# First attention layer: two heads of a chunk per job, score calls alternating between row halves and value calls between column halves

## What is computed

```python
# 16 query heads of 64 in 4 groups, one key and value head each; blocks of 128 queries
s_loc = einsum(q, k_of_3_blocks) * scale      # previous, own and next block, |distance| <= 128
s_loc = where(mask, s_loc, -inf)
s_ctx = einsum(q, k_context) * scale          # 256 context keys
p = softmax_with_sink(concatenate([s_loc, s_ctx]), sink)   # the sink's column is dropped after
ox = einsum(p[..., :384], v_of_3_blocks) + einsum(p[..., 384:], v_context)
# context queries attend to the context keys alone, with the sink
yx = (ox * silu(gx)) @ w_out                  # the same for the context
```

## Time and profile before

| | us |
|---|---|
| median of 3 runs | 3017.63 |
| lowest and highest run | 3004.48 to 3023.93 |
| the profiled execution | 3006.76 |
| its span, first to last instruction | 3005.4 |
| TensorE busy in the span | 2782.4 (93%) |
| DVE busy | 1707.1 (57%) |
| ACT busy | 1022.9 (34%) |

### The profile page before, as it was taken

How to read it: one execution, slowest core, us unless ns; L and a number is a source line. 1 busy time by engine, 2 the same in 40 slices (tenths; PEclk the granted TensorE clock), 3 DMA queues, 4 the chain that set the end, 5 groups by cost and what they waited for, 6 DMA issues and landing times.

```text
span 3005.4 us, 33845 instructions
## 1 busy us (share of the span) xinstructions
PE 2782.4 (93%) x12834; PEld 2170.3 (72%) x12834; DVE 1707.1 (57%) x3509; ACT 1022.9 (34%) x1662; POOL 319.8 (11%) x219
## 2 busy tenths in 40 slices
PE   6779999999999989999999996999999967999997
PEld 4657888988888879999999963986444655544445
DVE  4759777666666646767775454213555443154453
ACT  3222333333333323333333333222444332244442
POOL 0110344440000012212220000000000000000000
PEclk9989999999999999999999998998999988999998
DMA  5435444445656688989996520111000111100001
GB/s 214 154 112 192 166 145 146 142 162 196 223 199 220 210 288 294 312 283 313 311 313 224 183 77 21 50 59 33 1 1 1 35 35 57 58 24 16 9 1 56
DMA packets 147553, 415.95 MB, mean 138 GB/s; under 512 B 13568, under 2 KB 75136, under 8 KB 144448
## 3 DMA queue, kind: packets, MB, share of 16 engines
q1 hardware_dynamic: 128960, 346.67, 33.6%
q0 software_dynamic: 18432, 67.12, 6.6%
HBM read 352.62 MB, written 60.82 MB: 138 GB/s over the span
## 4 chain that ended last, share of the span: by engine, by line
PE 85%; issue 6%; DVE 5%; ACT 2%; POOL 2%; DMA 0%; SPq 0%; DVEq 0%; ACTq 0%; POOLq 0%
PE psum L447 7%; PE psum L449 7%; PE psum L448 7%; PE psum L334 6%; PE psum L336 6%; PE psum L335 6%; PE psum L326 6%; PE psum L328 6%; PE psum L327 6%; PE psum L420 4%; PE psum L564 3%; PE psum L707 3%; PE psum L557 2%; PE psum L677 2%; PE psum L318 2%
## 5 line engine op out<-in xcount | busy, mean ns | idle before, releaser
L1074 DVE TENSOR_TENSOR weights_low<-arena,weights_high 128x1024 fp32r<-128x1024 f32 x290 | 355.1, 1225 | 568.6 <-ACT weights_high L756 568.0
L756 ACT ACTIVATE weights_high<-arena 128x1024 fp32r<-128x1024 f32 x355 | 374.6, 1055 | 581.6 <-PE psum L449 416.3
L334 PE MATMUL psum<-x_high,weights_high 128*128 128x448 f32 x1024 | 381.5, 373 | 16.4 <-DVE weights_low L1074 9.2
L447 PE MATMUL psum<-hidden_high,weights_high 128*128 128x448 f32 x1024 | 374.6, 366 | 1.9 <-issue 1.9
L335 PE MATMUL psum<-x_low,weights_high 128*128 128x448 f32 x1024 | 375.1, 366 | 0.0
L336 PE MATMUL psum<-x_high,weights_low 128*128 128x448 f32 x1024 | 375.1, 366 | 0.0
L449 PE MATMUL psum<-hidden_high,weights_low 128*128 128x448 f32 x1024 | 373.9, 365 | 0.0
L448 PE MATMUL psum<-hidden_low,weights_high 128*128 128x448 f32 x1024 | 373.9, 365 | 0.0
L326 PE MATMUL psum<-x_high,weights_high 128*128 128x512 f32 x776 | 318.5, 410 | 39.9 <-DVE x_low L1088 20.9
L327 PE MATMUL psum<-x_low,weights_high 128*128 128x512 f32 x776 | 309.7, 399 | 0.0
L328 PE MATMUL psum<-x_high,weights_low 128*128 128x512 f32 x776 | 309.2, 398 | 0.0
(11 more groups left out here) (213 smaller groups left out, 4172.3 us busy)
## 6 DMA issues: line engine op xcount, KB each, us to landing
arena<-in_stream SPq DMA_DIRECT2D x227, 512.0 KB, 3.5
arena<-in_v_rows SPq DMA_DIRECT2D x128, 512.0 KB, 4.9
hidden<-arena SPq DMA_DIRECT2D x128, 224.0 KB, 2.7
router<-arena SPq DMA_DIRECT2D x14, 2048.0 KB, 8.3
arena<-hidden SPq DMA_DIRECT2D x128, 224.0 KB, 5.2
arena<-router SPq DMA_DIRECT2D x16, 1792.0 KB, 13.7
arena<-in_ada_w SPq DMA_DIRECT2D x48, 512.0 KB, 3.5
arena<-in_pair_w SPq DMA_DIRECT2D x8, 576.0 KB, 3.8
```

The source lines that it names most:

```text
L334: PE.matmul(bank[b][:, 0:N], wh[u % 2][:, k, :], xh[:, k, PICKED:T], start=k == 0, stop=False)
L447: PE.matmul(out, wh[w][:, n, :], hh[:, r, :], start=e == 0, stop=False)
L756: ACT.activation(wh[u % 2], slots[u % RING], AF.Copy).then_inc(*tick("weights_high", u))
L1074: DVE.tensor_tensor(wl[u % 2], slots[u % RING], wh[u % 2].bitcast(F32), ALU.subtract).then_inc(*tick("weights", u))
```

## The change

The jobs are dealt anew: jobs j and j + 1 are the two heads of a chunk at one query tile. `a_scores(j)` issues for both heads the context keys, then the near keys, then the masks, with each call in the other row half than the call before, and signals once at the end. It waits for both exponentials of the pair before, since each head now owns one score area. `a_turn(j)` transposes for both heads, after the scores of the next pair and the value pieces, the first four tiles of a head into bank 4 or 5 and the fifth into bank 7. `a_weigh(i, piece)` issues a piece for both heads, that is for partitions 0 to 63 and 64 to 127 of the output in turn; pieces 0 and 1 come with tile 1, 2 and 3 with tile 2, 4 and 5 with tile 3, 6 and 7 with tile 5. Pieces 6 and 7 write bank 6 and so wait for the gate of the first 512 queries. There are four probability buffers in place of three and two sets of `local_t` and `far_t` per chunk. ACT makes both exponentials of the next pair before the copies of this one; with three near tiles the context part is copied in two instructions. DVE normalises a pair, then takes the maxima of the next; the sink is copied for tile 0 alone; the gates are taken in two parts at different times. The second attention layer keeps its order.

```diff
@@ -216,12 +216,13 @@
     tmp = area(90, T)
     qr = [columns_at(8 * T + c * TC, TC) for c in range(5)] + [columns_at(72 * T + c * TC, TC) for c in range(2)] + [
         columns_at(88 * T, TC)]
-    prob = [columns_at(first * T, 641) for first in (36, 38, 46)]
-    local_t = [area(48, 4 * 3 * P), area(54, 4 * 3 * P)]
-    far_t = [area(51, 2, TC), area(57, 2, TC)]
+    prob = [columns_at(first * T, 641) for first in (36, 38, 46, 90)]
+    local_t = [[area(48, 4 * 3 * P), area(54, 4 * 3 * P)], [area(25, 4 * 3 * P), area(60, 4 * 3 * P)]]
+    far_t = [[area(51, 2, TC), area(57, 2, TC)], [area(28, 2, TC), area(68, 2, TC)]]
     mask_r = rounded("mask_rounded", 24, T)
     SC = [psum[:, 0:2 * T], psum[:, 2 * T:4 * T]]
     PT = psum[:, 4 * T:6 * T]
+    A_PT = [bank[4], bank[5]]
     def a_job(j):
-
-        head, t = divmod(j, TC // P)
-        return head // 2, head % 2, t
+        i, rest = divmod(j, 2 * (TC // P))
+        return i, rest % 2, rest // 2
 
...
-    A_PIECES = [0, 2, 2, 2, 1, 1]
+    A_PIECES = [(), (0, 1), (2, 3), (4, 5), (), (6, 7)]
...
         def a_scores(j):
-            i, half, t = a_job(j)
+            i, _, t = a_job(j)
             p = i % 2
-            rows = slice(64 * half, 64 * half + 64)
-            qs = qr[i][rows, t * P:(t + 1) * P]
             lo, tiles = a_tiles(t)
-            sc = SC[j % 2]
-            if j >= 2:
+            both = [(SC[half], slice(64 * half, 64 * half + 64)) for half in range(2)]
+            if j:
                 PE.wait_ge(*at("exped", ("a", j - 2)))
-            if j == 0:
+                PE.wait_ge(*at("exped", ("a", j - 1)))
+            else:
                 PE.wait_ge(*at("mask_r", 0))
                 for n in range(8):
                     PE.wait_ge(*at("roped", ("q", n)))
+            for sc, rows in both:
+                last = PE.matmul(sc[:, T:TC], qr[i][rows, t * P:(t + 1) * P], kt[rows, p, T:TC], start=True, stop=True)
             if t < NT:
                 first = tiles[0]
-                PE.matmul(sc[:, lo:T], qs, kt[rows, p, first * P:(tiles[-3] + 1) * P], start=True, stop=False)
                 skip = (first - t + 1) * P
-                PE.matmul(sc[:, lo:T], mask_r[:, 3 * P:4 * P], mask_r[:, skip:skip + T - lo], start=False, stop=True)
-            PE.matmul(sc[:, T:TC], qs, kt[rows, p, T:TC], start=True, stop=True).then_inc(*tick("scored", ("a", j)))
+                for sc, rows in both:
+                    PE.matmul(sc[:, lo:T], qr[i][rows, t * P:(t + 1) * P], kt[rows, p, first * P:(tiles[-3] + 1) * P],
+                              start=True, stop=False)
+                for sc, rows in both:
+                    last = PE.matmul(sc[:, lo:T], mask_r[:, 3 * P:4 * P], mask_r[:, skip:skip + T - lo], start=False,
+                                     stop=True)
+            last.then_inc(*tick("scored", ("a", j)))
+
+
+        def a_turn(j):
+            n = len(a_tiles(a_job(j)[2])[1])
+            if j:
+                PE.wait_ge(*at("prob_t", ("a", j - 2)))
+                PE.wait_ge(*at("prob_t", ("a", j - 1)))
+            for half in range(2):
+                PE.wait_ge(*at("normed", ("a", j + half)))
+                for b in range(n):
+                    out = A_PT[half][:, b * P:(b + 1) * P] if b < 4 else bank[7][:, half * P:(half + 1) * P]
+                    last = PE.transpose(out, prob[(j + half) % 4][:, b * P:(b + 1) * P], K("ident"))
+            last.then_inc(*tick("prob_turned", ("a", j)))
 
...
-        def a_weigh(head, piece):
-            i, half = head // 2, head % 2
-            kv = 2 * (i % 2) + half
-            rows = slice(64 * half, 64 * half + 64)
-            local, far = local_t[head % 2], far_t[head % 2]
+        def a_weigh(i, piece):
             if piece == 0:
-                PE.wait_ge(*at("prob_t", ("a", head * 6 + 5)))
-                if i and half == 0:
-                    PE.wait_ge(*at("a_gated", (i - 1, 0)))
-            if piece == 6 and i and half == 0:
-                PE.wait_ge(*at("a_gated", (i - 1, 1)))
-            if piece < 2 or piece >= 6:
-                j = piece % 2
-                v = vt[:, 4 + j, kv * 64:(kv + 1) * 64]
-                if piece < 2:
-                    PE.matmul(bank[6][rows, :], v, far[:, j, 0:T], start=j == 0, stop=False)
+                for half in range(2):
+                    PE.wait_ge(*at("prob_t", ("a", 12 * i + 10 + half)))
+                if i:
+                    PE.wait_ge(*at("a_gated", (i - 1, 1)))
+            elif piece == 6:
+                PE.wait_ge(*at("a_gated", (i, 0)))
+            for half in range(2):
+                kv = 2 * (i % 2) + half
+                rows = slice(64 * half, 64 * half + 64)
+                local, far = local_t[i % 2][half], far_t[i % 2][half]
+                if piece < 2 or piece >= 6:
+                    j = piece % 2
+                    v = vt[:, 4 + j, kv * 64:(kv + 1) * 64]
+                    if piece < 2:
+                        last = PE.matmul(bank[6][rows, :], v, far[:, j, 0:T], start=j == 0, stop=False)
+                    else:
+                        last = PE.matmul(bank[6][rows, 0:C], v, far[:, j, T:TC], start=j == 0, stop=j == 1)
                 else:
-                    last = PE.matmul(bank[7][rows, 0:C], v, far[:, j, T:TC], start=j == 0, stop=j == 1)
-                    if j == 1:
-                        last.then_inc(*tick("weighed", ("a", head)))
-            else:
-                j = piece - 2
-                t0, t1 = max(0, j - 1), min(NT, j + 2)
-                cols = local[:, j * 3 * P + (t0 - j + 1) * P:j * 3 * P + (t1 - j + 1) * P]
-                PE.matmul(bank[6][rows, t0 * P:t1 * P], vt[:, j, kv * 64:(kv + 1) * 64], cols, start=False, stop=j == 3)
+                    j = piece - 2
+                    t0, t1 = max(0, j - 1), min(NT, j + 2)
+                    cols = local[:, j * 3 * P + (t0 - j + 1) * P:j * 3 * P + (t1 - j + 1) * P]
+                    last = PE.matmul(bank[6][rows, t0 * P:t1 * P], vt[:, j, kv * 64:(kv + 1) * 64], cols, start=False,
+                                     stop=j == 3)
+            if piece in (5, 7):
+                last.then_inc(*tick("weighed", ("a", i, piece // 7)))
 
         a_scores(0)
-        a_scores(1)
-        for j in range(A_JOBS):
-            head, t = divmod(j, TC // P)
-            turn("a", j, prob, len(a_tiles(t)[1]))
+        for j in range(0, A_JOBS, 2):
+            i, _, t = a_job(j)
             if j + 2 < A_JOBS:
                 a_scores(j + 2)
-            if head:
-                for piece in range(sum(A_PIECES[:t]), sum(A_PIECES[:t + 1])):
-                    a_weigh(head - 1, piece)
+            if i:
+                for piece in A_PIECES[t]:
+                    a_weigh(i - 1, piece)
+            a_turn(j)
         for piece in range(8):
-            a_weigh(15, piece)
+            a_weigh(7, piece)
 
...
         def a_turn(j):
             i, half, t = a_job(j)
-            head = 2 * i + half
             lo, tiles = a_tiles(t)
             near = len(tiles) - 2
-            ACT.wait_ge(*at("prob_turned", ("a", j)))
-            if t == 0 and head >= 2:
-                ACT.wait_ge(*at("weighed", ("a", head - 2)))
+            local, far, pt = local_t[i % 2][half], far_t[i % 2][half], A_PT[half]
+            if half == 0:
+                ACT.wait_ge(*at("prob_turned", ("a", j)))
+                if t == 0 and i >= 2:
+                    ACT.wait_ge(*at("weighed", ("a", i - 2, 1)))
             if near:
                 first = tiles[0] * 2 * P + (t + 1) * P
-                where = local_t[head % 2][:, first:first + near * 2 * P].rearrange("p (n c) -> p n c", c=2 * P)[:, :, 0:P]
-                ACT.activation(where, PT[:, 0:near * P].rearrange("p (n c) -> p n c", c=P), AF.Copy)
-            ACT.activation(far_t[head % 2][:, :, t * P:(t + 1) * P],
-                           PT[:, near * P:(near + 2) * P].rearrange("p (n c) -> p n c", c=P), AF.Copy).then_inc(
-                               *tick("prob_t", ("a", j)))
+                where = local[:, first:first + near * 2 * P].rearrange("p (n c) -> p n c", c=2 * P)[:, :, 0:P]
+                ACT.activation(where, pt[:, 0:near * P].rearrange("p (n c) -> p n c", c=P), AF.Copy)
+            there = far[:, :, t * P:(t + 1) * P]
+            if near < 3:
+                last = ACT.activation(there, pt[:, near * P:(near + 2) * P].rearrange("p (n c) -> p n c", c=P), AF.Copy)
+            else:
+                ACT.activation(there[:, 0, :], pt[:, 3 * P:4 * P], AF.Copy)
+                last = ACT.activation(there[:, 1, :], bank[7][:, half * P:(half + 1) * P], AF.Copy)
+            last.then_inc(*tick("prob_t", ("a", j)))
 
         a_exponents(0)
         a_exponents(1)
-        for j in range(A_JOBS):
-            a_turn(j)
+        for j in range(0, A_JOBS, 2):
             if j + 2 < A_JOBS:
                 a_exponents(j + 2)
+                a_exponents(j + 3)
+            a_turn(j)
+            a_turn(j + 1)
 
...
```

(32 more changed lines are left out.)

21 lines of the change are left out of this document (10 added, 11 removed).

## The result

| | before | changed |
|---|---|---|
| median of the runs beside each other | 3020.17 us (3004.48 to 3023.93, 4 runs) | 2934.45 us (2925.97 to 2941.94, 4 runs) |
| profiled execution | 3006.76 | 2934.38 |
| first score pass to last gate, in it | 288.5 | 215.8 |

The ratio is 0.9729, 95% interval 0.9695 to 0.9763: faster by 2.7%.

The account below looks back on a forecast made before the run. TensorE's queue was taken to bound the stage; six chunks (-42.6), chunk 0 (-1.6) and the end (-7.5) gave -51.7 us with full overlap, taken as -47 from the 3017.6 median: 2970 us, range 2948 to 3003.

Parts of the forecast that it names:

- What bounds the kernel, and the change from TensorE to the loop: First attention stage: TensorE's queue bounds before; afterwards scores, maxima, exponentials and back through one score buffer set most steps.
- the number of slots that overlapped passes take: Score and value passes of a head pair: four calls of two passes take five slots instead of eight.
- the upper bound: Most overlap thought possible: a call's last pass runs beside the next call's first, giving 26.7 us per chunk against 33.78.
- The 4.7 us that I took off the full overlap: Whole stage: allowance for weight loads shown at calls, taking the full-overlap total of -51.7 us to -47.
- The six chunks: From value group to value group: each chunk 26.7 us instead of 33.78, together -42.6 us.
- Chunk 0: First score pass to first value group, without values to hide the loop, at 1.2 GHz: 52.6 against 54.2 us, -1.6.
- The end: From the value group of chunk 7 to the last gate: 24.2 us against 31.7, -7.5.
- The offset to the median: Whole run: before's profiled execution took 3006.8 us against a median of 3017.6; the saving was subtracted from that median.
- (a): Rival: passes of opposite halves do not overlap at all; +3 us, 3020; chance 0.11.
- (b): Rival: only one kind of half, rows or columns, overlaps; about -30 or -20 us, 2988 to 2998; chance 0.09.
- (c): Rival: clock falls in each chunk's thin stretch (tiles 4, 5, 0), 5.5 us a chunk, 3004, or 2985 at half; chance 0.12.
- (d): Rival: the stage stays at 1.2 GHz, a chunk some 43.5 us; +65 us, 3083; chance 0.06.

Follow-up runs that it names:

- e1: Changed kernel with the score calls written head by head (context and near of head 0, then of head 1) instead of alternating: 2935.57 us.
- e2: Changed kernel with a tile's value calls written head by head instead of alternating: 2939.13 us.
- e5: Changed kernel plus four products of 512 columns, results unread, ahead of the first score pass: 2941.34 us.
- e6: Changed kernel plus four unread products ahead of the first score pass and two more in each step of chunk 0: 2935.44 us.
- e9: Changed kernel with a signal per head, value pieces spread over all six steps, and unread products at the start and in chunk 0: 2928.07 us.
- e11: The changed kernel run once more, unaltered, for a second trace: runs of 2929.63 to 2958.86 us, the trace being that of the longest.
- e7: Changed kernel with the second head's score passes made to wait until the first head's have ended: 3022.85 us.

## Why the prediction was wrong in size

**What bounds the kernel, and the change from TensorE to the loop: right.** The loop that I read from the earlier trace rows came out to within 0.05 us. From the end of the block to the next context pass it is 4.93 - 1.73 = 3.20 at tile 0 (3.15 put), 4.63 - 1.50 = 3.13 at tile 5 (3.16) and 2.63 - 0.63 = 2.00 at tile 4 (2.04). The waits stand where I put them, released by ACT's exponential. One wait that I had not put is ahead of the transposes of tile 4, 0.71 behind ACT's copy (L976), and lies inside the loop's time.

**The term that was mis-sized: the number of slots that overlapped passes take.** A slot is the time of one pass. I called five slots for eight passes the upper bound, from the assumption that only the last pass of a call runs beside the first of the next. Measured are four: the two passes of each pair start 7 to 42 ns apart at a full clock, and e1 and e2 show that their calls need not be neighbours in the program. So my bound was none. A block is 0.63, 1.50 or 1.73 us, not 0.84, 1.71 or 2.17, and values 0 and 1 are 1.87, not 2.28. With four slots my own steps give 1.73 + 3.15 = 4.88, 1.73 + 1.86 + 1.25 = 4.84, 1.50 + 2.77 = 4.27, 0.63 + 1.22 + 1.03 = 2.88, 0.63 + 2.04 = 2.67 and 1.50 + 3.16 = 4.66, in all 24.2, and the trace has 24.23 where I put 26.7. In six chunks that is 6 x 2.5 = 15 us of the miss. The 4.7 us that I took off the full overlap (-47 for -51.7), for weight loads shown at each call, were not there either (value passes of one half follow each other at 0.43 us, as the stream alone would have it). The Trainium skill (TensorE: Matmul & The Clock Gate, Part 3, on packing small matmuls) says that matmuls of different strips run concurrently, which 7 ns between two starts confirms. Its rule that a weight load overlaps only when its rows differ does not hold here: the two heads' value weights have the same rows, and their loads are hidden (one runs from 2166.796 to 2166.933, within the pass from 2166.794 to 2167.386).

**The six chunks.** They took 150.0 us between first and last value group, against 202.7. At 24.2 each it would have been 145.4. The clock gave back 4.6 us. So this part is -52.7, put at -42.6.

**Chunk 0: the sign right, the size wrong.** 42.7 us, put at 52.6. I had it at 1.2 GHz all through, for I read from the earlier trace rows that only value passes end the slow phase. The row of after has 0.67: the clock rose at 2088.6, in the transposes behind a block, before any value pass. It fell and rose twice more, and the thin steps of tiles 3 and 4 ran at 2.4 GHz (2.62 each where I put 3.6).

```profile
2074.90:2088.60 13.70, 9.24 (x31) 6.02 (x32) 6.44 (x18) 4.43 (x12) 0.00 (x0) 0.50 0.00 0
2088.60:2092.00 3.40, 1.50 (x15) 1.30 (x15) 3.01 (x8) 2.27 (x7) 0.00 (x0) 1.00 0.00 0
```

The rest is slots: a full step at 1.2 GHz took 6.48, not 7.15. This part is -11.5, put at -1.6.

**The end.** 23.2 us from the last chunk's value group to the last gate, put at 24.2: -8.5, put at -7.5. The stage's miss of 25.7 us is then 10.1 in the chunks, 9.9 in chunk 0, 1.0 here and the 4.7 taken off.

**The offset to the median.** The profiled execution of before lay 10.9 us below the median, and I carried this over. That of after took 2934.38, its own median. This made the other 10 us of the miss beside the stage's (-72.7 in place of -47). Two parts vary most from execution to execution. One is the front: in the thirteen traces of kernels with the change it ends between 2073.3 and 2086.6 us, with the same code in it but for the four products at its end in e5, e6 and e9 (without those three, 2073.3 to 2085.9). The windows from 1200 to 1600 us of the changed kernel's two traces, the first with its front at 2073.8, the second at 2084.6:

```profile
1200.00:1600.00 400.00, 400.00 (x1975) 370.74 (x1974) 281.07 (x343) 126.12 (x165) 80.77 (x76) 1.00 0.90 304
```

```profile
1200.00:1600.00 400.00, 400.00 (x1937) 363.35 (x1937) 276.04 (x337) 122.93 (x162) 81.00 (x76) 1.00 0.87 299
```

The second has got 38 matmuls less far by 1600 us, with 299 GB/s moved in place of 304. What makes the transfers slower in some executions was not tried. The other part is the clock in the stage: 209.2 to 229.5 us for the same work. The code behind the stage varies less, 642.5 to 647.1 us. The profile of before had a short front (2074.1). That of after had one too, but its stage was 6 us over the 209.5 of the reordered kernels. If a stage like theirs is the usual one, which one trace each can't show, the change is worth about 288.5 - 209.5 = 79 us, near the 84 to 86 between the medians. That the stage of before varies too cannot be told from its one trace.

**The rivals.** (a) and (b) fell: there is overlap in both kinds. (c) is real in kind, and I had it at 5.5 us a chunk for one in eight. It is 3.1, and came twice in the six chunks of the first trace and in all six of e11's. It lies elsewhere than I put it: the steps of tiles 4, 5 and 0 kept 2.4 GHz (2.63, 4.62 and 4.93), and it was the block and the value passes behind them that ran at 1.2, so values don't end a fall at once. How often other executions have it, only their times hint at: one of six was 20 us longer than the rest. The Trainium skill (TensorE: Matmul & The Clock Gate, on a second failure of the clock) has the clock swing when the engine idles between groups of matmuls. The traces agree in part: there are 2.16 us of wait ahead of each of e11's six falls, and the same wait stood ahead of 23 steps of the six traces that were not slow. A wait of that length is not enough by itself, and what else decides is open. (d) did not come: no chunk behind chunk 0 ran wholly at 1.2 GHz. One end of the range does not follow from its own terms: a full overlap on a run of 3004 gives 3004.5 - 51.7 = 2952.8, not 2948. The measured time lies below both.

## What to carry to other kernels

When small float32 passes in opposite halves of the array are issued for two independent outputs, count each pair as one pass, also where another call stands between the two in the program. A wait between them undoes it. And then look at once for what bounds next, here a loop through one score buffer, where a copy of 0.16 us or a signal that comes one mask pass late is paid in full in the steps that the loop sets. A gap that the faster engine now has in every round can bring its clock down behind it. Spreading the work that is free to move over the gaps is worth more than the same work in lumps. Here it took 0.5 us off a chunk (23.81 to 23.29) and most of the long wait; three traces without a fall agree with it keeping the clock, and don't prove it.

## What was not expected of the hardware

- Passes of opposite halves start 7 ns apart, or 13 when their calls are apart in the program (36 and 42 from the second score pair on). They start out of the program's order: the second head's context passes run before the first head's near passes that stand ahead of them (e1). Only a wait kept them apart (e7).
- The same code took 2929.63 to 2958.86 us in six executions, the longest with a fall of the clock in each of its six chunks, each behind the 2.16 us wait. With a wait of 0.83 there was none in 18 chunks, and with 1.99 none in six.
- The clock rose in chunk 0 on score passes of half the array, masks and transposes alone, before any value pass.
